# Two edits of program order in a fused decoder trunk: a copy ahead of a square on ScalarE, and two transpose steps ahead of a projection on TensorE

## The chip, the core and the metric

The kernel runs on one core of a Trainium2 chip. The metric is the device time of one execution in microseconds (us). Three executions of the kernel before took 1684.36, 1684.06 and 1680.19 us; their median is 1684.06 us.

## The reference

The program computes one inference step of a decoder trunk with two layers, for 256 prompt tokens and 32 sample tokens (8 sequences of 4), so 288 columns in all, with a model width of 1024. Layer 0 is a Mamba-2 mixer beside sliding-window attention and a dense SwiGLU. Layer 1 is an RWKV-7 time mixing and a top-2-of-8 mixture of experts. The change lies in the RWKV-7 mixer, of which this is the part that matters:

```
r = xr @ wr;  k = xk @ wk;  v = xv @ wv
kk = hs(k * kk_coef)
kk = kk / max(sqrt(sum(kk * kk, axis=-1)), 1e-12)        # per head of 64
k = hs(k * (1 + (a - 1) * ka))
# a recurrence over the tokens with state S (per head 64 x 64):
sa = S @ (-kk);  S = S * w + sa * (kk * a) + v * k;  y = S @ r
y = groupnorm(y) + sum(r * k * rk) * v
out = (y * g) @ wo
```

The kernel doesn't run the recurrence token by token. It works on chunks, and inverts for each chunk and head a triangular matrix (I minus a strictly lower part) by doubling, in five levels.

## The kernel before

Activations are held feature-major: a tile is 128 features by 288 tokens, and a 1024-wide tensor is 8 such tiles (`KT` is 8). A projection to one output tile is a sum over 8 input tiles in one PSUM bank; in float32 each of these 8 products runs as two instructions on TensorE, so one output tile is 16 rows of the trace. There are 8 PSUM banks, handed out in turn to numbered stages. `take(g)` makes TensorE wait until stage g's bank was read by the one who used it 8 stages earlier; `full(engine, g)` makes an engine wait for TensorE, and `emptied(engine, g)` for the reader.

Each engine has its own program, and executes it strictly in the order in which it is written. Two orders matter here.

**The k projection.** TensorE's program (line 2711 and on) is: for t = 0 to 7, `column` of Rk(t) (8 products, wk times the mixed input), and for t of 1 and more behind it `squared_norm(t - 1)` (stage KN(t-1)): one product of a block matrix of ones with the squares of kk's tile t-1, which sums them per head. Then come the columns Rr(0) to Rr(7) of the r projection, with KN(7) behind Rr(0). ScalarE copies Rk(t) out of PSUM (line 1286), VectorE multiplies it by the coefficient (line 1933, signal `kk_raw`), ScalarE squares the product (line 1282, signal `kksq_ready`), TensorE waits for that signal ahead of KN, and VectorE takes the sum out of PSUM (line 1922). The loop at lines 1279 to 1287 writes ScalarE's order: the square of tile t-1, then the copy of Rk(t).

**The core list.** From line 556 on, a list `core` of steps is filled, and TensorE, VectorE and ScalarE all walk it, each doing its own part of a step. The steps near the change are: Rv(t), the v projection's output tile t (8 products; ScalarE copies it out at line 1313); BO(t), one product that sums r*k*rk per head (VectorE multiplies it by v at line 1978, scales it at line 1980, and prepares a later one with `bonus` at line 1948); X(0), the triangular products of the first head group, which VectorE masks (line 1994); M0(0), VectorE alone, which makes from X the start of the inverse in two halves, each by a multiply (line 2003) and an add (line 2005, signal `m0_ready`); T(0,0,q), four transposes of half q of that start (line 2777), which wait for `m0_ready` q + 1; LY, the first product of a doubling level, which needs GpSimd's masked rows (line 935) and the copied-out transposes. The same list numbers the stages, so that a step's place also decides its PSUM bank.

SyncE loads the weights; for the mixture of experts (line 811) it waits until slots come free by TensorE's progress.

Of the kernel before, what the change touches and what calls it, by code (L numbers as in the profile page):

```python
# [10 lines left out]
ACT = mybir.ActivationFunctionType  # L11
# [117 lines left out]
def decoder_trunk(nc, a, out):  # L129
    with ExitStack() as ctx:  # L130
# [5 lines left out]
        def sem(name):  # L136
            if name not in sems:
                sems[name] = ctx.enter_context(nc.semaphore(name))
            return sems[name]
# [42 lines left out]
        def area(n):  # L182
            o = pos[0]
            pos[0] += n
            assert pos[0] <= ARENA, (pos[0], ARENA)
            return ar[:, o:o + n]
# [77 lines left out]
        vT = area(KT * T).rearrange("p (k t) -> p k t", t=T)  # L264
# [6 lines left out]
        cum, pinv = [ar[:, A4_at + i * KT * T:A4_at + (i + 1) * KT * T].rearrange("p (k t) -> p k t", t=T) for i in range(2)]  # L271
# [134 lines left out]
        def stage(name, n):  # L406
            assert name not in base
            base[name] = order[0]
            order[0] += n
# [132 lines left out]
        def step(name, *which):  # L542
            core.append((name, which))
            n = {"X": 2, "A": 2, "M0": 0, "sA": 4, "sX": 2, "sZ": 2, "sU": 2, "sM": 0, "sE": 0, "WP": 0}.get(name, 1)
            stage((name, *which), n)
# [15 lines left out]
        step("M0", 0)  # L561
        step("Rv", 5)
        step("BO", 4)
        step("Rv", 6)
        step("T", 0, 0, 0)
        step("T", 0, 0, 1)
        step("BO", 5)
        for g in range(4):
            for lv in range(1, 6):
# [89 lines left out]
        def bank(g):  # L659
            return ps[:, g % 8, :]  # L660

        def full(eng, g):

            eng.wait_ge(sem(f"bank_full{g % 8}"), g // 8 + 1)
# [4 lines left out]
        def freesem(g):  # L669
            return sem(f"bank_free{g % 8}")  # L670
# [70 lines left out]
        def _(sp):  # L741
# [7 lines left out]
            def load_ffn_down(c):  # L749
# [3 lines left out]
                sp.dma_start(ring[:, o + GU:o + SLOT], a["ffn_w"][c][:, GU:SLOT]).then_inc(sem(f"ffn_down_loaded{c % RING}"), 16)  # L753

            for n, (name, _, src, w) in enumerate(items):
                if n == 0:
                    continue
# [260 lines left out]
        def _(act):  # L1018
            A = nc.scalar.activation
# [58 lines left out]
            for name, which in first:  # L1078
# [57 lines left out]
                elif name in ("K", "Q"):  # L1136

                    t = which[0]
# [105 lines left out]
            def own_share(n):  # L1244

                mrow = (1, 4, 5, 2, 0, 3)[n]
                full(act, users[n - 2])
                for k in range(KT):
                    if n == 2:
                        act.wait_ge(sem("h_tile"), KT + k + 1)  # L1250
                    A(xi[n % 2][:, k, :], h[:, k, :], ACT.Copy, scale=ommu[:, 8 * mrow + k:8 * mrow + k + 1]).then_inc(sem("act_tile"), 1)  # L1251
# [25 lines left out]
            lora_out("g", gT, None)  # L1277
            load_functions(LN_EXP)
            for t in range(KT + 1):
                if t:  # L1280
                    act.wait_ge(sem("kk_raw"), t)
                    A(pinv[:, t - 1, :], vT[:, t - 1, :], ACT.Square).then_inc(sem("kksq_ready"), 1)
                if t < KT:
                    g = base[f"Rk{t}"]
                    full(act, g)
                    A(k1[:, t, :], bank(g)[:, 0:T], ACT.Copy).then_inc(freesem(g), 1)
            own_share(5)
            act.wait_ge(sem("kn_max"), KT)
            for t in range(KT):
# [25 lines left out]
            for name, which in core:  # L1315
                g = base[(name, *which)]
                if name == "Rv":
                    t = which[0]
# [32 lines left out]
                elif name == "LY":  # L1351
                    q = which[2]
                    out_of(g, Yi[:, 4 * q:4 * q + 4, :], bank(g).rearrange("p (h t) -> p h t", t=P))
                    if which[0] == 0 and which[1] > 1:
                        t = 2 * (which[1] - 2) + q
# [139 lines left out]
        def _(dve):  # L1495
# [476 lines left out]
            for name, which in core:  # L1972
# [88 lines left out]
                elif name == "GV":  # L2061
                    n = which[0]
                    ks, ts, _, rsd = gn_unit(n)
                    emptied(dve, base["GM", n])
                    dve.wait_ge(sem("head_rs"), 18 + n + 1)
# [1179 lines left out]
```

## Time and profile before

| what | us |
|---|---|
| median of three executions | 1684.06 |
| profiled execution, its own time | 1684.36 |
| its span, first to last instruction | 1682.8 |
| TensorE matmul busy in it | 1650.8 (98%) |
| VectorE busy | 1172.6 (70%) |
| ScalarE busy | 915.0 (54%) |
| GpSimd busy | 145.1 (9%) |

The k projection begins at 534.18 us of the span and the v projection at about 612 us; the two places of the change lie at 545 to 577 us and at 631 to 636 us. The mixture of experts takes the last 780 us or so. The granted TensorE clock has a mean of 0.989 of 2.4 GHz; it stands at 1.00 outside a few short stretches. Busy time of TensorE counts the pipelined length of matmuls, so that a share of 98% says that it rarely stands still, not that it is at its peak.

### The profile page before, as it was taken

What the parts mean: (1) busy time and instruction counts of PE and PEld (TensorE: products, weight loads), DVE (VectorE), ACT (ScalarE), POOL (GpSimd) and SP (SyncE); (2) the same over time, 40 slices, a digit from 0 to 9 for tenths busy, and PEclk for the clock granted to TensorE, in tenths of its full rate; (3) what the DMA queues carried; (4) which work ended last, traced back from release to release, by engine and by line L of the source; (5) the groups of instructions that cost most, each with busy time, mean ns of one, the idle gap of its engine ahead of it and who ended that gap; (6) DMA issues with size and microseconds to landing.
All of it is one profiled execution on the core that took longest, in us unless ns stands there. A gap on an engine that the chain in (4) does not pass through costs nothing.

```text
span 1682.8 us, 25536 instructions
## 1 busy us (share of the span) xinstructions
PE 1650.8 (98%) x9976; PEld 1372.4 (82%) x9976; DVE 1172.6 (70%) x1512; ACT 915.0 (54%) x1190; POOL 145.1 (9%) x180
## 2 busy tenths in 40 slices
PE   9999999999999999999999999999999999999999
PEld 7766687999997778998866887878788887878787
DVE  4663732766767645443556979798887979898897
ACT  3352532533427425333435767687776767687774
POOL 1104000000000023222032000000000000000101
PEclk9999889999999999999899999999999999999999
DMA  8922433544423220000156989798997979898993
GB/s 342 390 109 100 201 150 152 225 150 151 150 95 145 101 100 1 2 2 2 58 200 245 427 332 428 313 419 355 377 412 319 428 307 424 347 386 350 380 426 127
DMA packets 41096, 405.02 MB, mean 241 GB/s; under 512 B 4784, under 2 KB 5072, under 8 KB 11664
## 3 DMA queue, kind: packets, MB, share of 16 engines
q1 hardware_dynamic: 34336, 372.64, 54.9%
q0 software_dynamic: 6672, 31.14, 4.6%
q8 instruction: 63, 1.03, 0.2%
q14 instruction: 25, 0.20, 0.0%
HBM read 379.49 MB, written 26.30 MB: 241 GB/s over the span
## 4 chain that ended last, share of the span: by engine, by line
PE 90%; DVE 4%; DMA 2%; ACT 2%; issue 1%; POOL 0%; DVEq 0%; ACTq 0%; SPq 0%; POOLq 0%
PE ps L2317 86%; DMA ring<-in_moe_w 1%; PE ps L3089 1%; PE ps L2777 1%; DVE rest_ring L2124 1%; DMA arena<-in_moe_w 1%; PE ps L2725 1%; DVE arena L1668 0%; ACT arena L1251 0%; DVE arena L1681 0%; ACT arena L1264 0%; PE ps L3042 0%; PE ps L2519 0%; DVE arena L1756 0%; POOL ring L924 0%
## 5 line engine op out<-in xcount | busy, mean ns | idle before, releaser
L2317 PE MATMUL ps<-head,hsel 128*128 128x512 f32 x1408 | 458.1, 397 | 2.8 <-DVE rest_ring L2124 2.8
L2317 PEld LDWEIGHTS ps<-head,hsel 128*128 128x128 f32 x1408 | 264.6, 188 | 61.4 <-DVE rest_ring L2124 7.8
L2124 DVE TENSOR_TENSOR rest_ring<-ring,head 128x2048 fp32r<-128x2048 f32 x128 | 291.1, 2285 | 13.7 <-ACT head L1403 13.7
L2317 PE MATMUL ps<-arena,ring 128*128 128x288 f32 (+9 forms) x1408 | 255.8, 347 | 1.2 <-ACT arena L1257 1.2
L1403 ACT ACTIVATE head<-ring 128x2048 fp32r<-128x2048 f32 x128 | 243.1, 1913 | 20.7 <-DMA ring<-in_moe_w 20.6
L2317 PEld LDWEIGHTS ps<-arena,ring 128*128 128x128 f32 (+4 forms) x1408 | 199.3, 189 | 52.4 <-issue 7.7
L2317 PE MATMUL ps<-rest_ring,hsel 128*128 128x512 f32 x512 | 199.8, 390 | 0.0
L2317 PE MATMUL ps<-head,actT_split 128*128 128x512 f32 x512 | 169.1, 394 | 7.4 <-issue 5.6
L2317 PE MATMUL ps<-rest_arena,head 128*128 128x288 f32 x704 | 174.8, 296 | 0.0
L2317 PE MATMUL ps<-rest_arena,rest_ring 128*128 128x288 f32 x528 | 155.6, 295 | 0.0
L2317 PE MATMUL ps<-h,ring 128*128 128x288 f32 (+2 forms) x624 | 133.5, 371 | 1.8 <-DVE h L1513 1.8
L2317 PEld LDWEIGHTS ps<-h,ring 128*128 128x128 f32 (+2 forms) x624 | 99.6, 176 | 35.3 <-issue 8.9
L2317 PEld LDWEIGHTS ps<-rest_arena,head 128*128 128x128 f32 x704 | 122.6, 188 | 0.1
L2317 PEld LDWEIGHTS ps<-head,actT_split 128*128 128x128 f32 x512 | 96.1, 188 | 31.6 <-issue 8.3
L2118 DVE TENSOR_TENSOR rest_ring<-ring,head 128x2048 fp32r<-128x2048 f32 x48 | 109.7, 2285 | 9.7 <-ACT head L1398 9.6
L2317 PE MATMUL ps<-arena 64*64 64x64 f32 (+11 forms) x1194 | 103.2, 289 | 9.8 <-DVE arena L1701 4.0
L2124 DVE TENSOR_TENSOR rest_arena<-arena,head 128x1024 fp32r<-128x1024 f32 (+1 forms) x64 | 110.3, 1751 | 2.0 <-ACT head L1403 1.7
L2317 PEld LDWEIGHTS ps<-rest_ring,hsel 128*128 128x128 f32 x512 | 96.5, 188 | 18.2
L2317 PE MATMUL ps<-hsel,head 128*128 128x288 f32 x352 | 103.9, 295 | 0.0
L1579 DVE TENSOR_TENSOR x<-x,ps 128x288 f32<-128x288 f32 x110 | 48.2, 452 | 77.7 <-PE ps L2317 77.4
L1403 ACT ACTIVATE head<-arena 128x1024 fp32r<-128x1024 f32 (+1 forms) x64 | 92.5, 1486 | 14.7 <-DMA arena<-in_moe_w 14.5
L2317 PE MATMUL ps<-rest_ring,actT_split 128*128 128x512 f32 x256 | 99.8, 390 | 0.0
(387 smaller groups left out, 2476.0 us busy)
## 6 DMA issues: line engine op xcount, KB each, us to landing
ring<-in_moe_w SPq DMA_DIRECT2D x64, 2048.0 KB, 12.2
ring<-in_moe_w SPq DMA_DIRECT2D x64, 1024.0 KB, 8.2
arena<-in_moe_w SPq DMA_DIRECT2D x24, 2048.0 KB, 11.3
arena<-in_moe_w SPq DMA_DIRECT2D x24, 1024.0 KB, 6.9
ring<-in_ffn_w SPq DMA_DIRECT2D x11, 2048.0 KB, 7.6
ring<-in_ffn_w SPq DMA_DIRECT2D x11, 1024.0 KB, 4.9
moe_rows<-arena POOLq DMA_DIRECT2D x1, 6656.0 KB, 34.0
ring<-in_w_in SPq DMA_DIRECT2D x2, 3072.0 KB, 13.0
```

The costliest lines, as they stand in the source:

```text
L1403: A(mhead[c % 2][:, o:o + w], mslot[s][:, o:o + w], ACT.Copy).then_inc(sem("gu_head"), 1)
L1579: V.tensor_tensor(x[:, m, :], x[:, m, :], bank(g)[:, 0:T], ALU.add).then_inc(freesem(g), 1)
L2118: V.tensor_tensor(mrest[s][:, GU:SLOT], mslot[s][:, GU:SLOT], down_head(c).bitcast(F32), ALU.subtract).then_inc(sem("dn_split"), 1)
L2124: V.tensor_tensor(mrest[s][:, o:o + w], mslot[s][:, o:o + w], mhead[c % 2][:, o:o + w].bitcast(F32), ALU.subtract).then_inc(sem("gu_split" ...
L2317: return nc.tensor.matmul(o, l, r, start=start, stop=stop, skip_group_check=skip)
L2725: ins = nc.tensor.transpose(b[0:rows, i * P:(i + 1) * P], src[:, 4 * hf + i, t0:t0 + rows], ident)
L2777: ins = nc.tensor.transpose(b[:, n * P:(n + 1) * P], (Mi if lv else Mti)[gg % 2][:, 4 * q + n, :], ident)
L3089: ins = nc.tensor.transpose(turned(c)[:, u * P:(u + 1) * P], actm[c % 2][:, u * P:(u + 1) * P], ident)
```

## The change

Two edits. In the list `core`, the two steps T(0,0,0) and T(0,0,1) come ahead of Rv(6) instead of behind it. In ScalarE's loop over the k projection, the copy of Rk(t) comes ahead of the square of tile t-1 instead of behind it. No instruction is added or taken away.

```
@@ the list of steps
         step("Rv", 5)
         step("BO", 4)
-        step("Rv", 6)
         step("T", 0, 0, 0)
         step("T", 0, 0, 1)
+        step("Rv", 6)
         step("BO", 5)
@@ ScalarE, the k projection
             for t in range(KT + 1):
-                if t:
-                    act.wait_ge(sem("kk_raw"), t)
-                    A(pinv[:, t - 1, :], vT[:, t - 1, :], ACT.Square).then_inc(sem("kksq_ready"), 1)
                 if t < KT:
                     g = base[f"Rk{t}"]
                     full(act, g)
                     A(k1[:, t, :], bank(g)[:, 0:T], ACT.Copy).then_inc(freesem(g), 1)
+                if t:
+                    act.wait_ge(sem("kk_raw"), t)
+                    A(pinv[:, t - 1, :], vT[:, t - 1, :], ACT.Square).then_inc(sem("kksq_ready"), 1)
```

ScalarE in the k projection, before. A row that reads `ps` and waits for a bank_full is the copy of an Rk tile; a row that waits for kk_raw is the square.

```order
L1286 ACTIVATE arena<-ps 128x288 [waits bank_full6]
L1282 ACTIVATE arena<-arena 128x288 [waits kk_raw]
L1286 ACTIVATE arena<-ps 128x288 [waits bank_full7]
L1282 ACTIVATE arena<-arena 128x288 [waits kk_raw]
L1286 ACTIVATE arena<-ps 128x288 [waits bank_full1]
L1282 ACTIVATE arena<-arena 128x288 [waits kk_raw]
```

The same place after the change, where the copy is at line 1283 and the square at line 1286:

```order
L1283 ACTIVATE arena<-ps 128x288 [waits bank_full6]
L1283 ACTIVATE arena<-ps 128x288 [waits bank_full7]
L1286 ACTIVATE arena<-arena 128x288 [waits kk_raw]
L1283 ACTIVATE arena<-ps 128x288 [waits bank_full1]
L1286 ACTIVATE arena<-arena 128x288 [waits kk_raw]
L1283 ACTIVATE arena<-ps 128x288 [waits bank_full3]
```

The first square stood ahead of the copy that waits for bank 7 (Rk(1)); now it stands behind it. The same holds for each square but the last, which has no copy left to stand behind.

TensorE around T(0,0,q), difference with the waits. `cst,ring` 128x128 rows are the transposes, the `arena,ring` 128x288 rows are Rv(6), the `arena,cst` rows are BO(4) and BO(5), and the `ring` rows are LY.

```order
 L2317 MATMUL ps<-arena,cst 128x288 [waits bank_free2,bonus_ready]
-L2317 MATMUL ps<-arena,ring 128x288 [waits bank_free3,slot_loaded2]
-L2317 MATMUL ps<-arena,ring 128x288 x7
+L2777 MATMUL ps<-cst,ring 128x128 [waits bank_free3,m0_ready]
+L2777 MATMUL ps<-cst,ring 128x128 x3
 L2777 MATMUL ps<-cst,ring 128x128 [waits bank_free4,m0_ready]
 L2777 MATMUL ps<-cst,ring 128x128 x3
-L2777 MATMUL ps<-cst,ring 128x128 [waits bank_free5,m0_ready]
-L2777 MATMUL ps<-cst,ring 128x128 x3
+L2317 MATMUL ps<-arena,ring 128x288 [waits bank_free5,slot_loaded2]
+L2317 MATMUL ps<-arena,ring 128x288 x7
```

The eight products of Rv(6) moved from ahead of both waits for m0_ready to behind them. ScalarE's copy of Rv(6) moved behind its two copies of the transposes in the same way, and the three stages swapped their banks.

## Rows read from the trace of the kernel before

**Rows 1.** The page, busy time: engine, us, share of span, instructions.

```profile
PE 1650.8 (98%) x9976; PEld 1372.4 (82%) x9976; DVE 1172.6 (70%) x1512; ACT 915.0 (54%) x1190; POOL 145.1 (9%) x180
```

**Rows 2.** Chain that ended last, 534 to 700: start us, us, what.

```profile
534.18 100.98 PE ps L2317 x426
636.04 8.96 PE ps L2317 x54
```

**Rows 3.** Timeline of TensorE, 510 to 576: start, us, line, out<-in, count, [idle before].

```profile
534.18 11.91 PE L2317 MATMUL ps<-arena,ring 128*128 128x288 f32 x48 [1.24 <-ACT arena L1257]
545.92 0.65 PE L2317 MATMUL ps<-arena,cst 128*128 128x288 f32 x2
...
550.29 0.65 PE L2317 MATMUL ps<-arena,cst 128*128 128x288 f32 x2
```

**Rows 4.** Timeline of ScalarE, 528 to 576.

```profile
533.66 0.47 ACT L1257 ACTIVATE arena<-ps 128x288 f32<-128x288 f32 x1
...
546.13 0.41 ACT L1286 ACTIVATE arena<-ps 128x288 f32<-128x288 f32 x1 [2.52 <-PE ps L2317]
547.04 0.44 ACT L1282 ACTIVATE arena<-arena 128x288 f32<-128x288 f32 x1 [0.51 <-DVE arena L1933]
```

**Rows 5.** Timeline of ScalarE, 582 to 590, a copy and an SBUF operation behind it.

```profile
588.81 0.41 ACT L1298 ACTIVATE arena<-ps 128x288 f32<-128x288 f32 x1 [2.70 <-PE ps L2317]
589.11 0.43 ACT L1301 ACTIVATE arena<-arena 128x288 f32<-128x288 f32 x1
```

**Rows 6.** Timeline of VectorE, 528 to 576, one tile's multiply by the coefficient.

```profile
551.01 0.37 DVE L1933 TENSOR_SCALAR arena<-arena,vec 128x288 f32<-128x288 f32 x1 [1.40 <-ACT arena L1286]
```

**Rows 7.** Timeline of TensorE, 605 to 665.

```profile
630.63 0.65 PE L2317 MATMUL ps<-arena,cst 128*128 128x288 f32 x2
631.12 4.04 PE L2317 MATMUL ps<-arena,ring 128*128 128x288 f32 x16
635.00 1.04 PE L2777 MATMUL ps<-cst,ring 128*128 128x128 f32 x8
635.87 0.65 PE L2317 MATMUL ps<-arena,cst 128*128 128x288 f32 x2
636.36 2.00 PE L2317 MATMUL ps<-ring 128*128 128x128 f32 x16
...
645.71 1.06 PE L2317 MATMUL ps<-ring 128*128 128x128 f32 x8
```

**Rows 8.** Timeline of VectorE, 600 to 665.

```profile
631.38 1.47 DVE L2005 TENSOR_TENSOR ring<-ring,cst 128x512 f32<-128x512 f32 x1
...
634.09 0.69 DVE L2005 TENSOR_TENSOR ring<-ring,cst 128x512 f32<-128x512 f32 x1
...
636.64 0.45 DVE L1978 TENSOR_TENSOR arena<-arena,ps 128x288 f32<-128x288 f32 x1 [0.51 <-PE ps L2317]
```

**Rows 9.** Timeline of ScalarE, 600 to 665, the transposes copied out.

```profile
635.64 1.08 ACT L1313 ACTIVATE ring<-ps 128x512 f32<-128x512 f32 x2
```

**Rows 10.** Timeline of GpSimd, 600 to 665, masked rows of level 2.

```profile
639.33 2.14 POOL L935 TENSOR_TENSOR ring<-ring,cst 128x512 f32<-128x512 f32 x2
```

**Rows 11.** Windows: stretch, length, busy us (count) by engine, clock, DMA share, GB/s.

```profile
645.00:800.00 155.00, 152.48 (x1706) 140.04 (x1706) 68.31 (x115) 60.67 (x115) 41.15 (x36) 1.00 0.01 2
...
850.00:930.00 80.00, 77.24 (x360) 53.27 (x360) 52.18 (x106) 33.13 (x44) 23.75 (x21) 1.00 0.63 248
930.00:1680.00 750.00, 740.41 (x3351) 603.73 (x3349) 646.88 (x480) 543.78 (x473) 23.86 (x20) 1.00 0.88 364
```

**Rows 12.** Waits of the DMA queue of SyncE: us in total, times, longest.

```profile
SPq L811 <- PE ps L2317: 545.3, 77, 10.7
```

**Rows 13.** Windows of three stretches, columns as in rows 11.

```profile
83.00:108.00 25.00, 20.98 (x138) 15.89 (x136) 21.11 (x67) 20.47 (x27) 0.00 (x0) 1.00 0.38 148
184.00:198.00 14.00, 10.43 (x60) 7.83 (x59) 8.76 (x32) 11.88 (x40) 0.00 (x0) 0.63 0.92 382
808.00:822.00 14.00, 14.00 (x127) 12.22 (x126) 8.53 (x15) 5.13 (x14) 0.00 (x0) 0.52 0.01 2
```

More of the change, by code:

```diff
@@ L563, in decoder_trunk @@
         step("BO", 4)
-        step("Rv", 6)
         step("T", 0, 0, 0)
         step("T", 0, 0, 1)
+        step("Rv", 6)
         step("BO", 5)
@@ L1279, in _ @@
             for t in range(KT + 1):
-                if t:
-                    act.wait_ge(sem("kk_raw"), t)
-                    A(pinv[:, t - 1, :], vT[:, t - 1, :], ACT.Square).then_inc(sem("kksq_ready"), 1)
                 if t < KT:
@@ L1286, in _ @@
                     A(k1[:, t, :], bank(g)[:, 0:T], ACT.Copy).then_inc(freesem(g), 1)
+                if t:
+                    act.wait_ge(sem("kk_raw"), t)
+                    A(pinv[:, t - 1, :], vT[:, t - 1, :], ACT.Square).then_inc(sem("kksq_ready"), 1)
             own_share(5)
```

## The prediction, made before the changed kernel ran

> **What bounds the kernel now.** I read the page's busy times first: TensorE is busy for 1650.8 of 1682.8 us, no other engine for more than 70% [rows 1]. So the question for each edit is whether TensorE stands still longer. The chain of waits says the same for the place of the change: from 534.18 on it runs for 100.98 us through TensorE's own instructions without one piece of another engine between them, and goes on so behind 636.04 [rows 2]. Nothing in this stretch waits for ScalarE, VectorE or GpSimd, so no reordering can gain there: TensorE has no gap to close. It can only lose, if an order makes TensorE wait. Then I read the timelines of the engines at the two places, for the moment at which each signal comes and the moment at which it would be needed.
>
> **The change, part by part.**
>
> *ScalarE's copy ahead of its square (the k projection).* Before, ScalarE copies Rk(1) out at 546.13 and squares tile 1 at 547.04, as soon as VectorE's product is there; the square ends at 547.48 [rows 4]. TensorE needs it for KN(1) at 550.29, behind Rk(2); from one KN to the next it is 4.37 us (545.92 to 550.29) [rows 3]. The slack is 2.8 us per tile.
>
> After, the square of tile t-1 stands behind the copy of Rk(t), and this copy waits for the end of Rk(t). But TensorE's next instruction behind Rk(t) is KN(t-1), which waits for that very square. So TensorE must stand still through the copy and the square. With the times of t = 1: KN(0) would start at 545.92 [rows 3]. The copy can't start earlier than it does, at 546.13, when the last product of Rk(1) has run out [rows 4]. The operation behind a copy starts 0.30 us after it (588.81 to 589.11) [rows 5]; the square takes 0.44 [rows 4]; TensorE starts 0.05 after the releasing operation ended (533.66 + 0.47 = 534.13 against 534.18) [rows 3, 4]. KN(0) starts at 546.13 + 0.30 + 0.44 + 0.05 = 546.92, which is 1.00 us late. TensorE also starts slowly behind a stop: the 48 instructions from 534.18 to 545.92 took 11.74 us, while 18 take 4.37 in the steady run, which makes 11.65 for 48; so 0.09 more [rows 3]. One stall is 1.09 us.
>
> How many: KN(0) to KN(6) each stand behind a column Rk(1) to Rk(7), so 7. KN(7) stands behind Rr(0), and its square is the one with no copy ahead of it: unchanged. 7 x 1.09 = 7.6 us. Nothing is taken off: VectorE's product for the square is long there, and VectorE, which reads KN(t-1) about 0.3 us later relative to the tile grid, waits 1.40 us for the copy in each tile [rows 6]. Bounds for one stall: at least 0.21 + 0.30 + 0.43 = 0.94, if release and restart cost nothing; at most 0.21 + 0.41 + 0.44 + 0.05 + 0.09 = 1.20, if copy and square don't overlap. That is 6.6 to 8.4 us; a gain is excluded because TensorE has no gap there. I take 7.6, since rows 5 are the same two operations back to back.
>
> *T(0,0,0) and T(0,0,1) ahead of Rv(6).* Before, TensorE runs Rv(6) from 631.12 to 635.00 and then the transposes, in 0.87 us, to 635.87 [rows 7]. VectorE makes the two halves of the start meanwhile: they are there at 631.38 + 1.47 = 632.85 and at 634.09 + 0.69 = 634.78 [rows 8]. Rv(6) thus covered both waits, with 0.2 us to spare. After, TensorE comes to T(0,0,0) at 631.12 and waits to 632.85 + 0.05 = 632.90; it does four transposes (half of 0.87, so 0.44), and waits for the second half to 634.83. Restart 0.09, transposes 0.44: 635.36. Rv(6) takes its 3.88 us, to 639.24; BO(5) then starts there instead of at 635.87. The cost is 3.37 us. X, which starts VectorE's work, is ahead of the change, and so is everything that GpSimd does beside it, so the two moments stay where they are relative to X. If VectorE's add took as long as its longest form in both halves (1.47 instead of 0.69), the cost would be 4.1; if both halves waited with no restart and no release cost, 3.2.
>
> Does something later repay it? The transposes are copied out earlier; that copy was at 635.64 [rows 9], and LY, which needs it, started at 636.36 straight behind BO(5) [rows 7]: no wait there to be removed. ScalarE copies Rv(6) out later, and BO(5), BO(6) on VectorE follow later, by 3.4 us like all behind them. What hangs on BO(5) is `bonus(7)` and behind it GpSimd's masked rows of level 2, which began at 639.33 and ended at 641.47 [rows 10]; they were needed at 645.71 [rows 7], 4.2 us later, and both ends shift together, since BO(5) on VectorE waits for TensorE (636.64, idle before it ended by TensorE) [rows 8]. The swapped PSUM banks were all last read by stages 8 earlier, which are over.
>
> *Behind 636.* The delay adds up to 11.0 us and has to pass through 1040 us more. TensorE's standstill there is small: 155 - 152.48 = 2.5 us in the rest of the recurrence, 2.8 us in 850 to 930, 9.6 us in the experts [rows 11], and these waits are for engines and transfers that are themselves started by TensorE's progress: the expert weights are requested when slots come free, where the queue waited 545.3 us for TensorE [rows 12]. A transfer that waits for a slot starts later by the delay, and gives nothing back.
>
> **Sum.** 7.6 + 3.4 = 11.0 us (bounds 9.8 to 12.5). The profiled execution took 1684.36 us with a span of 1682.8, and is 0.30 above the median. 1684.36 + 11.0 = 1695.4; against the median 1695.1. I say 1695.2 us, 0.66% longer.
>
> **The clock.** Where TensorE stopped again and again in the trace, in 83 to 108 (20.98 busy of 25), the granted clock stayed at 1.00, that is 2.4 GHz; in 184 to 198 (10.43 of 14) it fell to a mean of 0.63, that is for 0.37/0.5 of 14 = 10.4 us at the lower level of 1.2 GHz [rows 13]. The seven stalls leave TensorE busy for 4.37 of 5.46 us, 80%, near the first stretch (84%); the two waits ahead of Rv(6) leave about 1.0 us of work in 4.2, less than the second stretch has. The Trainium skill, page "TensorE: Matmul & The Clock Gate", section "A second HAM failure mode: psum-queue depth-cycling", says that frequent short stops between groups of matmuls make the clock swing between its two levels. The row of 83 to 108 speaks against that for stops of this share. By that rule the time would be that of the second rival below.
>
> **The rivals.**
>
> 1. *The clock falls less often elsewhere, and the kernel is not slower.* The trace has two stretches at the lower clock of 10.4 us and, at 808 to 822, of 0.48/0.5 of 14 = 13.4 us [rows 13]. What TensorE does at half clock takes twice as long, so they cost up to 5.2 and 6.7 us. If the second, behind the change, doesn't come when the work gets there 11 us later, the time is 1695.2 - 6.7 = 1688.5, within 0.3% of before; it decides for "not slower" if at least 5.9 us of low-clock cost go. For it: the three executions differ by 4.2 us though their work is the same. Against it: the stretch at 808 hangs on its own instructions, which stay as they are; a shift changes little of it. 6%.
> 2. *The clock falls in the added waits.* The standstill ahead of Rv(6) is denser than in 184 to 198. A fall of 10.4 us there, during Rv(6), BO(5), LY and Rv(7), costs 5.2 us: 1700.4. Against it: it is a single stop of 4 us behind 95 us of unbroken work. In the stalls of the k projection a fall over all 7 tiles would cost 7 x 4.37 = 30.6 us, but 83 to 108 speaks against that. 13%.
> 3. *The wait ahead of Rv(6) is given back*, because the other engines are 3.4 us ahead of TensorE from there on, and the 2.5 us of standstill to 800 shrink: 1693 at the least, or 1691.8 if all 3.4 go. For it: VectorE and ScalarE are busy with work of their own there. Against: they wait for TensorE at BO(5) and are back in step. 8%.
> 4. *The edit on ScalarE costs nothing*, because the square would be there in time, and only the 3.4 us remain: 1687.6. That would need KN(t-1) not to wait for a square behind the copy of Rk(t), which both engines' order excludes. 4%.
>
> **How the numbers follow.** The forecast has 69%, with a range of its own of 1692 to 1698 (the bounds of the sum, and some 2 us for the difference between executions). A difference under 0.3%, 5.05 us, can't be told from none here; the bound is 1689.1. Slower: the forecast, rivals 2 and 3, 90% less 1 for a fast set of executions, 0.89. Same: rivals 1 and 4 and that 1%, less a little, 0.10. Faster 0.01. The range of 8 in 10 reaches from 1689.5 to 1700.5, and leaves out most of rivals 1 and 4 and the upper part of rival 2.
>
> **What would show it.** In the trace after, the row of KN(0) should carry an idle time of about 0.8 us ended by ScalarE's square, seven times, with a distance of 5.46 us from one KN to the next. At 638.7 (631.12 + 7.6) TensorE should stand for 1.7 and then 1.4 us, both ended by VectorE's add. The chain of waits should run through ScalarE's copy and square at each of the seven. The experts should take as long as before. The prediction is wrong if the KN rows have no idle time, if the sum of idle in 534 to 650 grows by 11 us but the span doesn't, or if the clock in 545 to 660 is under 1.00.

## The result, and the profile after

| | before | after |
|---|---|---|
| median of five executions beside each other, us | 1683.29 | 1697.47 |
| lowest and highest of them | 1680.19, 1684.36 | 1694.51, 1703.2 |
| profiled execution, its own time | 1684.36 | 1697.79 |
| its span | 1682.8 | 1696.2 |
| mean granted clock in it | 0.989 | 0.987 |

The ratio is 1.0083, with a 95% interval of 1.0059 to 1.0105: the change makes the kernel slower by 14.2 us in these five, where 11.9 us were forecast against 1683.29 (1695.2; the working had 11.0 over the profiled 1684.36). Seventeen executions of the changed kernel, taken over all sessions, have a median of 1696.6 us, 54 of the kernel before, recorded beside the experiments below, one of 1683.65: 13.0 us.

The waits of the stretch from 534 to 660 us of the changed kernel, where TensorE is the one that waits (us in total, times, longest):

```profile
PE ps L2317 <- ACT arena L1286: 5.8, 7, 0.8
...
PE ps L2777 <- DVE ring L2005: 2.9, 2, 1.6
...
PE ps L2317 <- ACT arena L1257: 1.2, 1, 1.2
```

The third was there before [rows 3]. The first is new, seven times; so is the second, twice. Nothing else of weight has appeared. TensorE's timeline through the k projection shows the seven:

```profile
534.33 11.91 PE L2317 MATMUL ps<-arena,ring 128*128 128x288 f32 x48 [1.24 <-ACT arena L1257]
547.07 0.75 PE L2317 MATMUL ps<-arena,cst 128*128 128x288 f32 x2 [0.83 <-ACT arena L1286]
547.65 4.04 PE L2317 MATMUL ps<-arena,ring 128*128 128x288 f32 x16
552.53 0.75 PE L2317 MATMUL ps<-arena,cst 128*128 128x288 f32 x2 [0.83 <-ACT arena L1286]
...
579.85 0.75 PE L2317 MATMUL ps<-arena,cst 128*128 128x288 f32 x2 [0.83 <-ACT arena L1286]
580.43 4.04 PE L2317 MATMUL ps<-arena,ring 128*128 128x288 f32 x16
584.31 0.65 PE L2317 MATMUL ps<-arena,cst 128*128 128x288 f32 x2
```

Each KN row of two instructions has 0.83 us of idle ahead of it, ended by ScalarE's square at line 1286, and from one to the next it is 5.46 us (547.07 to 552.53), where it was 4.37 [rows 3]. The last row, KN(7) at 584.31, has no idle. On ScalarE the copy and the square stand together at the end of a tile, where before the copy of Rk(1) began at 546.13 and the square of tile 1 at 547.04 [rows 4]:

```profile
546.27 0.41 ACT L1283 ACTIVATE arena<-ps 128x288 f32<-128x288 f32 x1 [3.47 <-PE ps L2317]
546.58 0.43 ACT L1286 ACTIVATE arena<-arena 128x288 f32<-128x288 f32 x1
```

The copy starts 0.02 us after TensorE's last product ran out and the square 0.31 us behind it. The chain of waits of the same kernel (start, us, what) now goes through both, seven times over:

```profile
534.33 11.92 PE ps L2317 x48
546.25 0.02 issue
546.27 0.41 ACT arena L1283
546.68 0.34 ACT arena L1286
547.02 0.04 issue
547.07 4.65 PE ps L2317 x18
```

The other place, TensorE around the two transpose steps. It answers to [rows 7]:

```profile
638.47 0.65 PE L2317 MATMUL ps<-arena,cst 128*128 128x288 f32 x2
640.73 0.66 PE L2777 MATMUL ps<-cst,ring 128*128 128x128 f32 x4 [1.62 <-DVE ring L2005]
642.66 1.11 PE L2777 MATMUL ps<-cst,ring 128*128 128x128 f32 x4 [1.27 <-DVE ring L2005]
643.57 6.56 PE L2317 MATMUL ps<-arena,ring 128*128 128x288 f32 x16
649.97 0.65 PE L2317 MATMUL ps<-arena,cst 128*128 128x288 f32 x2
```

Both waits are there, at the forecast distance behind BO(4). But the sixteen instructions of Rv(6) now take 6.40 us to BO(5) instead of 3.88. The windows of that stretch tell why (columns as in rows 11; the third number from the end is the granted clock):

```profile
638.00:640.00 2.00, 1.12 (x5) 0.56 (x3) 1.97 (x2) 0.41 (x1) 2.00 (x2) 1.00 0.00 0
640.00:642.00 2.00, 0.66 (x4) 0.42 (x4) 1.97 (x3) 0.57 (x1) 1.33 (x2) 0.96 0.00 0
642.00:644.00 2.00, 1.34 (x5) 1.25 (x6) 1.92 (x4) 0.21 (x2) 0.00 (x0) 0.50 0.00 0
644.00:646.00 2.00, 2.00 (x6) 1.38 (x5) 0.00 (x0) 0.41 (x1) 1.54 (x2) 0.50 0.00 0
646.00:648.00 2.00, 2.00 (x6) 1.43 (x5) 0.00 (x0) 0.00 (x0) 0.00 (x0) 0.50 0.00 0
648.00:650.00 2.00, 2.00 (x9) 1.54 (x8) 0.00 (x0) 0.00 (x0) 0.00 (x0) 0.84 0.00 0
650.00:652.00 2.00, 2.00 (x17) 1.90 (x16) 1.24 (x3) 0.87 (x2) 0.00 (x0) 1.00 0.03 8
```

TensorE was busy for 1.12 and 0.66 of 2 us while it waited; from about 641.8 the clock was at its lower level of 1.2 GHz, for some 6.8 us as the windows add up, and it was back at 2.4 GHz before BO(5) began. The two profiles can now be laid beside each other, each from the first product of Rk(0):

| up to | before | after | more |
|---|---|---|---|
| KN(7) | 42.30 | 49.98 | 7.68 |
| BO(4) | 96.45 | 104.14 | 7.69 |
| BO(5) | 101.69 | 115.64 | 13.95 |

The last step of 6.26 us has two parts. At the higher clock the two waits with their restarts would make it 3.3 us: T(0,0,1) starts at 642.66, which is 3.70 us behind the end of BO(4) at 638.96 (its start and the 0.49 us that it takes in [rows 7]), its four transposes take 0.49 us (as in the run *filled* below, which keeps the clock up), and 0.87 us of transposes stood there before; 3.37 us were forecast. The other 2.9 us are work at the lower clock: 2.52 in Rv(6) (6.40 instead of 3.88) and 0.42 in the second transposes (0.91 instead of 0.49). Behind BO(5) little changes: from there to the end it is 1046.9 us before and 1046.2 after, 0.7 less, and Rk(0) began 0.15 us later; so the spans are 13.4 us apart.

### The profile page after: what moved, and what is told of

The parts are those of the page before. It is cut to its first block, busy times and chain, and to the rows that moved or that the text cites. A ratio compares the mean times of both kernels' runs of the same rounds, so it can differ in the third digit from the quotient of the medians.

```text
span 1696.2 us, 25536 instructions
## 1 busy us (share of the span) xinstructions
PE 1656.4 (98%) x9976; PEld 1372.8 (81%) x9976; DVE 1172.4 (69%) x1512; ACT 914.6 (54%) x1190; POOL 142.8 (8%) x180
## 4 chain that ended last, share of the span: by engine, by line
PE 90%; DVE 5%; ACT 2%; issue 1%; DMA 1%; POOL 0%; DVEq 0%; ACTq 0%; SPq 0%; POOLq 0%
PE ps L2317 86%; DVE rest_ring L2124 1%; DMA ring<-in_moe_w 1%; PE ps L3089 1%; PE ps L2777 1%; PE ps L2725 1%; DVE arena L1668 0%; ACT arena L1251 0%; DVE arena L1681 0%; ACT arena L1264 0%; PE ps L3042 0%; PE ps L2519 0%; DVE arena L1756 0%; POOL ring L924 0%; DVE arena L1542 0%
## 6 DMA issues: line engine op xcount, KB each, us to landing
arena<-in_moe_w SPq DMA_DIRECT2D x24, 2048.0 KB, 11.3
```

## The experiments

All were timed in five rounds beside executions of the kernel before. The ratios with their intervals are as recorded; they aren't the quotients of the two medians beside them, and differ from these by up to 0.0012. Executions of one kernel turned out to spread by up to 13.6 us (before: 1679.94 to 1691.19 in 54; changed: 1691.33 to 1704.91 in 17), and their mean granted clock goes along with that. So for each kernel I also give the time *at equal clock*: over all 148 executions of all kernels here, each compared with its own kernel's mean, time rises with the lost clock, (1 - mean clock) x span, by 0.78 us for each us, with a correlation of 0.97; the difference between two kernels' mean times less 0.78 times their difference in lost clock is an estimate of what the kernel itself costs, with a standard error of 0.2 to 0.4 us. In this measure the changed kernel is 11.1 us over the kernel before (1681.1 against 1670.0), and 1.6 of the 12.7 us between their mean times is lost clock (20.2 against 18.1 us per execution). The clock is recorded to a thousandth, which is 1.7 us of lost clock; single executions can't be taken further.

The measure takes a lost us to cost the same everywhere, and the profiles show that it doesn't. The fall at 184 to 198 in the profile before loses 0.37 x 14 = 5.2 us of clock. From the six instructions at 182.67 to the column at 205.91 TensorE takes 23.24 us there; in the run one_step below, which has the clock at 1.00 in that stretch, the same work takes 21.29 us (182.50 to 203.79). So this fall costs 1.95 us, 0.38 for each us lost, because TensorE waits for other engines in between: 1.00 and 0.74 us with the fall, 1.70 and 2.02 without it. Behind the two waits of the changed kernel 3.4 us lost cost 2.9. An edit that brings or removes a fall at one place can therefore be off by a us or two in this measure.

**Only ScalarE's loop changed** (only_copy). The changed kernel with the list of steps as before:

```
         step("BO", 4)
+        step("Rv", 6)
         step("T", 0, 0, 0)
         step("T", 0, 0, 1)
-        step("Rv", 6)
```

> Only the edit on ScalarE's loop is kept (copy of Rk(t) ahead of the square of tile t-1); the list of steps is as before. Theory (seven stalls of TensorE, one per KN(0) to KN(6), each 1.09 us, passed on in full): about 7.7 us more than before, KN rows 5.46 us apart, no stretch at the lower clock in 530 to 660 and so a spread of executions like that of before. Rival (the stalls themselves make the clock fall in some executions): more than 10 us over before in the median, with a mean clock lower than before's 0.989 by 0.002 or more.

Measured: 1690.51 against 1683.59 us, 1.0044 (1.0028 to 1.0060), so 6.9 us more; at equal clock 7.6. Lost clock was 17.3 us on the mean, not more than before's 18.1, so the stalls cost no clock. The profile had clock 1.00 in 534 to 665, and TensorE's rows:

```profile
546.45 0.75 PE L2317 MATMUL ps<-arena,cst 128*128 128x288 f32 x2 [0.83 <-ACT arena L1286]
547.04 4.04 PE L2317 MATMUL ps<-arena,ring 128*128 128x288 f32 x16
551.92 0.75 PE L2317 MATMUL ps<-arena,cst 128*128 128x288 f32 x2 [0.83 <-ACT arena L1286]
```

The theory holds, the rival falls. The spread (1687.71 to 1699.25, 11.5 us) is like that of the kernel before (11.3 us), as expected; what makes it lies elsewhere in the program.

**Only the list of steps changed** (only_steps, and a second time as only_steps_b):

```
         step("BO", 4)
-        step("Rv", 6)
         step("T", 0, 0, 0)
         step("T", 0, 0, 1)
+        step("Rv", 6)
```

> Only the edit in the list of steps is kept (both transpose steps ahead of Rv(6)). Theory (two waits for VectorE, 3.4 us, and in executions in which the clock falls behind them some 3 us more): 3.4 to 6.4 us over before in the median, and a profile in which BO(5) comes 3.4 us late where the clock stays at 1.00 and about 6.3 us late where it falls. Rival (the order costs 3.4 us alone and the extra 2.9 us of the changed kernel's profile come from the two edits together): 3.4 us, clock 1.00 in 630 to 655.

> The kernel with only the list of steps changed a second time, beside the others on one chip, since its first executions ran from 1687.4 to 1698.4 us and its profile had a fall of the clock behind the transposes that the theory puts down to the standstill. Theory: the profile shows a fall in 632 to 645 again, Rv(6) over 4.5 us, and the median is 5 to 8 us over before. Rival (the fall came by chance): Rv(6) takes 3.88 us, and the median is 3.4 to 5 us over before.

Measured: 1689.71 against 1683.59 us, 1.0042 (1.0026 to 1.0058), and the second time 1688.41 against 1683.70, 1.0031 (1.0019 to 1.0043): 6.1 and 4.7 us. At equal clock 4.1 and 3.7 us. TensorE in the two profiles, first only_steps, then only_steps_b:

```profile
633.23 0.66 PE L2777 MATMUL ps<-cst,ring 128*128 128x128 f32 x4 [1.62 <-DVE ring L2005]
635.16 1.04 PE L2777 MATMUL ps<-cst,ring 128*128 128x128 f32 x4 [1.27 <-DVE ring L2005]
635.99 5.39 PE L2317 MATMUL ps<-arena,ring 128*128 128x288 f32 x16
641.22 0.65 PE L2317 MATMUL ps<-arena,cst 128*128 128x288 f32 x2
```

```profile
630.55 0.66 PE L2777 MATMUL ps<-cst,ring 128*128 128x128 f32 x4 [1.62 <-DVE ring L2005]
632.48 0.93 PE L2777 MATMUL ps<-cst,ring 128*128 128x128 f32 x4 [1.27 <-DVE ring L2005]
633.21 5.50 PE L2317 MATMUL ps<-arena,ring 128*128 128x288 f32 x16
```

The waits are the same to a hundredth, 1.62 and 1.27 us. Rv(6) took 5.23 and 5.33 us: the clock fell behind the waits here too, for a shorter time than in the changed kernel. BO(5) is 5.02 and 5.01 us later behind BO(4) than before, so the fall costs 1.7 us here; 6.3 us late was expected where the clock falls, after the 2.9 us of the changed kernel's profile. So the fall doesn't need the other edit. The second median, 4.7 us over, missed the 5 to 8 us that I gave and lay in the rival's range, though the profile went against the rival; the medians alone don't tell a fall of 1.5 to 3 us from none.

**The waits filled with work** (filled; and after_filled, the same in the changed kernel). TensorE does products that are overwritten while it would stand still:

```
-                    if lv:
+                    b = take(g)
+                    if gg == 0 and lv == 0:
+                        for _ in range((3, 2)[q]):
+                            mm(b[:, 0:T], C("blk64"), h[:, 0, :])
+                    if lv:
                         emptied(pe, base["LM", gg, lv, q])
                     else:
                         pe.wait_ge(sem("m0_ready"), 2 * gg + q + 1)
-                    b = take(g)
```

> As the kernel with only the list of steps changed, and TensorE does five products whose results are overwritten (128x288, into the bank that the transposes write next) while it waits for VectorE: three ahead of T(0,0,0), two ahead of T(0,0,1), 2.4 us of work in 3.2 us of waiting. Theory (the extra cost is the clock, which falls because TensorE stands still): the clock stays at 1.00 behind the transposes, Rv(6) takes 3.88 us, and the kernel is 3.4 to 3.7 us over before, some 1 to 3 us under the kernel with only the steps changed. Rival (Rv(6) is slow for another reason, as contention of ScalarE, GpSimd or a late weight slot): Rv(6) takes 6.4 us here too.

> The changed kernel, and TensorE does five overwritten products while it waits for the two halves of the start (three and two, 128x288). Theory (of the changed kernel's cost 11.1 us are stalls and the rest, 1 to 3 us, is a fall of the clock behind the standstill ahead of Rv(6)): Rv(6) takes 3.88 us, clock 1.00 in 638 to 650 of the profile, and a median 10.5 to 12 us over before. Rival (the clock falls in many places by chance, and the standstill adds nothing to it): median as for the changed kernel, 12.5 to 14 us over before, whether or not the profile shows Rv(6) at full clock.

TensorE in the profile of filled:

```profile
631.44 1.62 PE L2317 MATMUL ps<-h,cst 128*128 128x288 f32 x6
633.22 0.66 PE L2780 MATMUL ps<-cst,ring 128*128 128x128 f32 x4 [0.16 <-DVE ring L2005]
633.72 1.14 PE L2317 MATMUL ps<-h,cst 128*128 128x288 f32 x4
635.16 0.66 PE L2780 MATMUL ps<-cst,ring 128*128 128x128 f32 x4 [0.30 <-DVE ring L2005]
635.65 4.05 PE L2317 MATMUL ps<-arena,ring 128*128 128x288 f32 x16
639.53 0.65 PE L2317 MATMUL ps<-arena,cst 128*128 128x288 f32 x2
```

The transposes start at the same moments as in only_steps (633.22 and 635.16), since VectorE sets them, but Rv(6) takes 3.88 us; in after_filled too (643.13 to 647.01). BO(5) comes 8.57 us behind BO(4) (630.96 to 639.53) against 5.24 before: 3.33 us more, the forecast's 3.37. The windows of 630 to 650 show the clock, first only_steps, then filled:

```profile
630.00:650.00 20.00, 17.11 (x85) 13.78 (x84) 9.36 (x14) 5.64 (x9) 8.24 (x8) 0.91 0.00 1
```

```profile
630.00:650.00 20.00, 19.53 (x110) 15.95 (x109) 10.84 (x16) 6.59 (x11) 8.23 (x8) 1.00 0.00 1
```

So it is TensorE's standing still, and not contention or a late slot, that makes Rv(6) slow: three profiles of three with both waits and without the products have it slow, two of two with the products have it at full clock, and the five of the kernels that lack one wait or both (before, only_copy, late_norm, one_step, before_filled) have a clock of 1.00 in 630 to 660. In the whole time this can't be seen. filled took 1689.60 against 1683.59 us, 1.0024 (1.0008 to 1.0040): 6.0 us over in the median where 3.4 to 3.7 were expected, like only_steps with 6.1 and 4.7. At equal clock it is 4.3 us over, against 4.1 and 3.7. after_filled took 1695.30 against 1683.70, 1.0067 (1.0055 to 1.0079): 11.6 us over in the median, inside the theory's 10.5 to 12. But it has six executions only, their mean (1697.2) isn't below that of the changed kernel (1696.9), and at equal clock it is 11.7 us over, against the changed kernel's 11.1. What the products save is less than what the clock does by chance in the rest; that much of the rival stands.

**TensorE's norm one tile later** (late_norm). ScalarE's loop stays changed, the list of steps is as before, and TensorE and VectorE do KN(t-2) where they did KN(t-1) (the stages are numbered in the same way):

```
                 column(base[f"Rk{t}"], "k", 3, t)
-                if t:
-                    squared_norm(t - 1)
+                if t > 1:
+                    squared_norm(t - 2)
```

> The edit on ScalarE's loop is kept, the list of steps is as before, and TensorE does KN(t-2) instead of KN(t-1) behind Rk(t) (KN(6) and KN(7) both behind Rr(0)); VectorE takes the sums out one tile later in the same way. Theory (the cost is only the distance between the square and its use, which is a whole tile again): no idle in the KN rows, within 0.3% of before (0 to 0.5 us over). Rival (copy ahead of square costs by itself, by VectorE or ScalarE getting out of step): some us over before remain.

Measured: 1684.51 against 1683.59 us, 1.0000 (0.9986 to 1.0014); at equal clock 0.1 us over before. ScalarE has the same order as in the changed kernel, copy ahead of square, and TensorE's KN rows have no idle:

```profile
549.83 0.65 PE L2319 MATMUL ps<-arena,cst 128*128 128x288 f32 x2
550.31 4.04 PE L2319 MATMUL ps<-arena,ring 128*128 128x288 f32 x16
554.19 0.65 PE L2319 MATMUL ps<-arena,cst 128*128 128x288 f32 x2
```

The order costs nothing by itself. What it costs is that the square's only user stands directly behind the product for which the copy ahead of it waits.

**Only the first transpose step moved** (one_step):

```
         step("BO", 4)
-        step("Rv", 6)
         step("T", 0, 0, 0)
+        step("Rv", 6)
         step("T", 0, 0, 1)
```

> As before, but only T(0,0,0) stands ahead of Rv(6); T(0,0,1) stays behind it. Theory (each wait adds by itself): T(0,0,0) waits 1.62 us for VectorE, T(0,0,1) not at all, BO(5) is 1.9 us late, and with a single stop the clock stays at 1.00 there, so 1.9 us over before, not to be told from no change. Rival (the step must stand behind Rv(6) as a pair, or the order of ScalarE's copies costs too): 3 us or more.

```profile
628.34 0.65 PE L2317 MATMUL ps<-arena,cst 128*128 128x288 f32 x2
630.60 0.66 PE L2777 MATMUL ps<-cst,ring 128*128 128x128 f32 x4 [1.62 <-DVE ring L2005]
631.10 4.05 PE L2317 MATMUL ps<-arena,ring 128*128 128x288 f32 x16
634.98 0.60 PE L2777 MATMUL ps<-cst,ring 128*128 128x128 f32 x4
635.41 0.65 PE L2317 MATMUL ps<-arena,cst 128*128 128x288 f32 x2
```

BO(5) is 7.07 us behind BO(4) instead of 5.24, so 1.83 us late, by one wait and one restart, and Rv(6) runs at full clock. Time: 1683.78 against 1683.70, 0.9994 (0.9983 to 1.0005); at equal clock 1.6 us over. Its executions happened to lose less clock (15.6 us), which hid the cost. The first wait alone makes 1.8 of the 3.4 us.

**Filled waits in the kernel before** (before_filled). Five such products where TensorE stands still in 184 to 194 us, the first of the two long falls of the clock [rows 13]. In the transposes:

```
                     j = which[0]
+                    if j == 0:
+                        b = take(g)
+                        for _ in range(3):
+                            mm(b[:, 0:T], C("blk64"), h[:, 0, :])
                     pe.wait_ge(sem("p_ready"), j + 1)
```

> The kernel before, with five overwritten products where TensorE stands still in 184 to 194 us of its trace: three ahead of the transposes of the first attention group (a wait of 1.66 us), one ahead of its output product (1.00 us) and one ahead of the third group's scores (0.74 us). Theory (the clock falls at 187 us because TensorE does little just ahead of it): clock 1.00 in 184 to 198, and up to 5 us less than before where TensorE's work at the lower clock set the pace, 2 us at the likeliest, since the other engines' waits lie between. Rival (the fall has another cause, as the small tiles, or the products come too late): clock 0.5 in 188 to 197 as before, time within 0.3% or up to 1 us more.

Measured: 1683.41 against 1683.70 us, 1.0008 (0.9995 to 1.0021), not to be told from no change. The profile had clock 1.00 in 184 to 198. But so had one_step, and only_steps_b, with nothing filled there (first before_filled, then one_step):

```profile
184.00:198.00 14.00, 11.05 (x77) 7.87 (x77) 10.11 (x35) 12.32 (x44) 0.00 (x0) 1.00 0.88 360
```

```profile
184.00:198.00 14.00, 8.43 (x67) 6.43 (x67) 10.18 (x33) 12.09 (x40) 0.00 (x0) 1.00 0.95 385
```

Of the ten profiles seven have the fall (0.63 to 0.76 in 184 to 198). So it comes in some executions and not in others, and one profile with it away shows nothing. The result is inconclusive on the cause. As to the time, there was less to win than the 5 us of the expectation, since the fall costs 1.95 us. At equal clock the kernel is 2.1 us over before, but the products cost nothing where they stand: from 183.11 to 204.40 the profile takes 21.29 us, as one_step does without them. The measure itself may make most of the 2.1 us (an estimate from the figures above: a kernel that never has this fall is credited with 0.78 x 5.2 = 4.1 us for a gain of 1.95, and seems up to 2.1 us too dear). What is left isn't explained.

## Why the prediction was right

The seven stalls and the two waits were foretold rightly, the clock behind them was not. The measured 1697.47 us lies between the forecast of 1695.2 and rival 2's 1700.4, and within the forecast's own range of 1692 to 1698 by 0.5 us. That it does so is partly luck: the fall of the clock that the sum left out was shorter than rival 2 had it.

*Nothing to gain.* Right: TensorE had no gap at either place, and no part of the change shortened anything [rows 2, 3, 7].

*Seven stalls of 1.09 us, 7.6 in all.* Right to 0.1 us. KN(7) came 7.68 us late, only_copy cost 7.6 us at equal clock (its profile, too, has clock 1.00 there), and the parts agree one by one: square 0.31 us behind the copy (0.30 taken), idle 0.83 us (0.8 foretold), distance 5.46 us (5.46 foretold), KN(7) without idle. late_norm shows that the stall is the distance between square and use.

*Two waits ahead of Rv(6), 3.37 us.* Right in the trace: T(0,0,0) 2.26 us behind BO(4) (2.27 taken), T(0,0,1) 4.19 us (4.20), and 3.33 us in all where the clock stayed up (filled). The idle times were 1.62 and 1.27 us, where 1.7 and 1.4 were foretold. only_steps measured 4.1 and 3.7 us at equal clock, 0.4 to 0.8 more than 3.3. The fall at that place could explain 0.4 of this (1.8 us lost in 630 to 650, at nearly 1 us each and not 0.78), but filled, whose profile has no fall there, measured 4.3 us. So up to 1.0 us between trace and whole time stays unexplained.

*Passed on in full.* Right: from BO(5) to the end the two profiles differ by 0.7 us, and at equal clock the whole kernel is 11.1 us over before where the traces have 7.7 + 3.3 = 11.0, which is closer than that measure is good for. Rival 3 (given back later) is out.

*The clock.* Half right. That the seven stalls leave it alone was right, in three profiles (1.00 in 534 to 600 in after, only_copy and after_filled). The rule of the Trainium skill, page "TensorE: Matmul & The Clock Gate", section "A second HAM failure mode: psum-queue depth-cycling", on short stops that swing the clock did not apply to these stops. For the standstill ahead of Rv(6) the forecast's sum put nothing, and the fall of the clock stood only as rival 2, with 13%. It came in all three profiles of a kernel with both waits and nothing in them: 0.83 in 640 to 660 of the changed kernel. By the prediction's own last sign ("if the clock in 545 to 660 is under 1.00") it was wrong here. This is the step that failed, and it is a term of 2.9 us in the changed kernel's profile, not the 5.2 us that rival 2 had: the fall lasted some 7 us and not 10.4. With it the profile's sum is 7.7 + 3.3 + 2.9 = 13.9 us, as BO(5) shows. Rival 2 named the mechanism and the row that spoke for it, and this should have weighed more: about 1.0 us of work in 4.2 is less than anything else in the trace has (the least in any 4.2 us of the trace before is 2.05, from 86, where the clock stayed at 1.00; so sparse work alone isn't shown to be the cause). The 10.43 us of busy time in 184 to 198, with which the prediction compared, are partly the low clock itself: the same work is 8.43 us of busy time at the higher clock (one_step).

*Rival 1* (falls of the clock elsewhere go away) didn't happen in the changed kernel's profile. The fall behind the change moved along with its work: the 48 us from 798 in the profile before and the 48 us from 812 in the one after both have a mean clock of 0.86, and the fall at 184 to 198 is in both (0.63 and 0.64). Its price for the latter, up to 5.2 us, was far above the 1.95 us that it costs. That falls come and go at all is a matter of chance between executions of any kernel, as 54 executions of the kernel before and the ten profiles show; nothing ties it to the shift. *Rival 4* is out by only_copy.

Still open: why a fall comes in some executions at 184 us and not in others, and how much of the 1.6 us of additional lost clock in the mean of the changed kernel is the one behind the waits, and the up to 1.0 us of filled. That would need many more executions.

## What to carry to other kernels

On an engine that works through its list in order, an operation that is put behind a wait inherits that wait; look for the first user of its result, and count the distance to it in instructions of the engine that sets the end. If the user stands directly behind what is waited for, the whole of copy, operation and release lies on the path, every time round the loop; if it stands a tile later, it costs nothing. A step whose input isn't ready belongs behind work that is, and when two short waits follow each other with hardly any work between, the clock has to be added to the price (here 1.7 to 2.9 us in the profiles). A comparison at equal clock is only as good as the price of a lost us at the place where the clock falls; look for that price in a profile without the fall.

## What the runs showed of the hardware

- The same program differs by 11 to 14 us between executions on one core (before: 1679.94 to 1691.19, changed: 1691.33 to 1704.91), and nearly all of it goes with TensorE's granted clock: 0.992 to 0.986 of mean clock go with 1680.0 to 1689.3 us. The Trainium skill, page "TensorE: Matmul & The Clock Gate", section "HAM oscillation — how this bites in real kernels", describes falls of the clock by waits for transfers. Here a fall also comes and goes at one place behind the same wait, as 184 to 198 us shows: 0.63 in the profile before, behind a wait of 1.66 us, and 1.00 in one_step, behind one of 1.67 us.
- What a fall costs depends on who sets the pace there: 5.2 us of lost clock cost 1.95 us at 184 to 198, where TensorE waits for other engines, and 3.4 us cost 2.9 behind the two waits, where TensorE stands still no more until BO(5).
- Two waits of 1.62 and 1.27 us with four transposes between them brought a fall to 1.2 GHz in three profiles of three; one wait of 1.62 us (one_step), and seven of 0.83 us, each with 4.6 us of work behind it, brought none.
- TensorE restarts behind a wait with 0.1 us of loss: the first KN instruction takes the row from 0.65 to 0.75 us.
